# Attention scores from stacked parts, with the row's minimum as the exponential's offset

## The reference, cut to what matters

```python
s = jnp.einsum('bnqkgd,bnskd->bnkgqs', qb, kb, preferred_element_type=jnp.float32) * (HEAD_DIM ** -0.5)
s = jnp.where(mask[None, :, None, None], s + bias, NEG_INF)
sink_col = jnp.broadcast_to(sink.astype(jnp.float32).reshape(B_KV_HEADS, grp, 1, 1), s.shape[:-1] + (1,))
p = jax.nn.softmax(jnp.concatenate([s, sink_col], axis=-1), axis=-1)[..., :-1]
o = jnp.einsum('bnkgqs,bnskd->bnqkgd', p.astype(vb.dtype), vb)
```

## Time and profile before

| | |
|---|---|
| median of 3 runs | 1834.66 us (1833.57 to 1834.83) |
| the profiled execution | 1834.38 us, span 1832.6 us |
| granted TensorE clock, mean | 0.948 |
| TensorE busy with matmuls | 1627.7 us, 89% |
| DVE busy | 1338.2 us, 73% |
| ACT busy | 930.8 us, 51% |

### The profile page before, as it was taken

One profiled execution on the slowest core, in us unless ns is written; L12 is line 12 of the kernel. 1 busy time (PEld: TensorE's weight loads), 2 busy tenths in 40 slices (PEclk: granted clock), 3 DMA queues, 4 the chain that ended last, 5 costly groups with the idle time before them and its releaser, 6 DMA issues. The chain is left out here.

```text
span 1832.6 us, 28264 instructions
## 1 busy us (share of the span) xinstructions
PE 1627.7 (89%) x8048; PEld 1277.8 (70%) x8049; DVE 1338.2 (73%) x2015; ACT 930.8 (51%) x1499; POOL 307.7 (17%) x312
## 2 busy tenths in 40 slices
PE   3999888986899999991799999999999999999950
PEld 2777667874567666671678888888888888888840
DVE  5578867894578888885758977785766866656938
ACT  2312362224676666631637766573554655444728
POOL 0000100000100111113121523213122322211213
PEclk9999898997899999995899999999999999999975
DMA  7657765225733333324787989878787888776657
GB/s 303 230 195 251 254 208 192 82 81 166 307 116 116 116 115 116 105 81 174 286 332 230 393 329 364 289 281 311 237 291 251 288 296 252 265 241 197 200 152 318
DMA packets 116608, 412.84 MB, mean 225 GB/s; under 512 B 11919, under 2 KB 48015, under 8 KB 87872
## 3 DMA queue, kind: packets, MB, share of 16 engines
q1 hardware_dynamic: 95792, 342.62, 49.5%
q0 software_dynamic: 19744, 68.20, 14.6%
q10 hardware_dynamic: 1008, 1.22, 0.2%
HBM read 333.29 MB, written 80.81 MB: 226 GB/s over the span
## 5 line engine op out<-in xcount | busy, mean ns | idle before, releaser
L2025 ACT CAST gate_up_hi<-gate_up_raw 128x1024 fp32r (+1 forms) x256 | 265.7, 1053 | 91.5 <-PE psum_up L1966 65.7
L2165 DVE TENSOR_TENSOR gate_up_lo<-gate_up_raw,gate_up_hi 128x1024 fp32r<-128x1024 f32 x256 | 300.4, 1219 | 11.6 <-ACT gate_up_hi L2025 2.5
L491 PE MATMUL proj_bank<-x_hi,w_hi 128*128 128x512 f32 x448 | 182.2, 407 | 22.8 <-DVE w_lo L603 16.0
L493 PE MATMUL proj_bank<-x_hi,w_lo 128*128 128x512 f32 x448 | 177.6, 396 | 0.0
L492 PE MATMUL proj_bank<-x_lo,w_hi 128*128 128x512 f32 x448 | 177.5, 396 | 0.0
L1961 PE MATMUL psum_gate<-gate_up_hi,x_hi 128*128 128x512 f32 x392 | 158.2, 404 | 7.8 <-DVE gate_up_lo L2165 3.9
L1975 PE MATMUL psum_y<-down_hi,h_hi 128*128 128x512 f32 x392 | 158.6, 405 | 4.7 <-DVE h_lo L2165 4.7
L2165 DVE TENSOR_TENSOR down_lo<-down_raw,down_hi 128x1024 fp32r<-128x1024 f32 x128 | 150.7, 1219 | 9.0 <-ACT down_hi L2033 5.2
L669 DVE SCALAR_TENSOR_TENSOR conv<-y_win,cw,conv 128x1008 f32<-128x1008 f32 (+1 forms) x120 | 154.0, 1283 | 3.0
L1962 PE MATMUL psum_gate<-gate_up_lo,x_hi 128*128 128x512 f32 x392 | 154.1, 393 | 0.0
L1976 PE MATMUL psum_y<-down_lo,h_hi 128*128 128x512 f32 x392 | 154.0, 393 | 0.0
(11 more groups left out here) (292 smaller groups left out, 3327.8 us busy)
## 6 DMA issues: line engine op xcount, KB each, us to landing
gate_up_raw<-in_w_gate_up SPq DMA_DIRECT2D x128, 1024.0 KB, 9.4
down_raw<-in_w_down SPq DMA_DIRECT2D x64, 1024.0 KB, 6.2
x_raw<-in_ada_w SPq DMA_DIRECT2D x16, 1024.0 KB, 4.8
w_raw<-in_w_in SPq DMA_DIRECT2D x28, 512.0 KB, 5.6
x_raw<-in_xT SPq DMA_DIRECT2D x16, 512.0 KB, 9.7
q_kept<-q_stage SPq DMA_DIRECT2D x32, 256.0 KB, 2.8
q_tile<-q_kept SPq DMA_DIRECT2D x16, 512.0 KB, 4.2
wo<-w_out_kept SPq DMA_DIRECT2D x8, 1024.0 KB, 13.3
```

Source lines behind the costliest of these rows:

```text
L491: mm(bank[:, :], w_hi[side][:, k, :], x_hi[m][:, k, :], start=(k == 0), stop=False)
L493: last = mm(bank[:, :], w_lo[side][:, k, :], x_hi[m][:, k, :], start=False, stop=(k == DC - 1))
L2025: nc.scalar.copy(gu_hi[:, k, :], raw_chunk(slot, k)).then_inc(gu_high_ready, 1)
L2165: return tt(out, raw, high.bitcast(F32), ALU.subtract)
```

## The change

1. **Negated, scaled queries.** The query weights and their bias are multiplied by -1/8 where the high and low parts are made, and the table of biases by -1 instead of 8. The scores come out as minus the true ones. DVE keeps the row's minimum, started from minus the sink, and that minimum is the exponential's offset as it stands; line 1371 goes.
2. **Stacked parts.** `k_all[:, g]` now holds the high part of key head g on its own 64 partitions and its low part on the other 64. The low parts get there over a new tile `k_low` and two DMAs per key unit. The query's high part is loaded into both halves of the partitions (`q_twice`), so that one matmul with 128 contraction rows gives high·high plus high·low. Low·high stays a matmul with 64 rows.
3. **The loads of the queries** become five DMAs a tile, 768 KB instead of one of 512 KB.
4. **ACT waits** for each head's own reading of scores, not for the pair's.
5. **Memory**: `mod_rows` lies in `conv_std`, `h2T` in `x_raw`; a wait at the end of the attention stands earlier.

```diff
+QUERY_CHUNKS = slice(2 * 5, 2 * 7)
+MINUS_SCALE = -HD ** -0.5
+def load_query(sp, io, keep, t):
+    landed = keep["q_landed"][t % 2]
+    for g in range(KV_HEADS):
+        for half in range(2):
+            sp.dma_start(keep["q_twice"][HD * half:HD * half + HD, t % 2, g].rearrange("p a b -> p (a b)").bitcast(F32),
+                         io["q"][t, HD * g:HD * g + HD, 0].rearrange("p a b -> p (a b)")).then_inc(landed, 16)
+    sp.dma_start(keep["q_low"][:, t % 2].rearrange("p a b -> p (a b)").bitcast(F32),
+                 io["q"][t, :, 1].rearrange("p a b -> p (a b)")).then_inc(landed, 16)
...
+            def spread_k(n):
+                h, p, m, side = unit_of(n)
+                cols = slice(HALF * (2 * h + m), HALF * (2 * h + m + 1))
+                sp.wait_ge(dve_emptied, units_up_to(n, EMPTIED_BY_DVE))
+                for g in range(KV_HEADS):
+                    other = HD * (1 - g)
+                    sp.dma_start(k_all[other:other + HD, g, cols].bitcast(F32), k_low[HD * g:HD * g + HD, :]
+                                 ).then_inc(k_spread, 16)
...
-                low(w_lo[side][:, :, :], w_raw[side][:, :, :], w_hi[side][:, :, :].bitcast(F32)).then_inc(w_low, 1)
+                if CHUNK_KINDS[p][side] == QUERY:
+                    stt(w_lo[side][:, :, :], w_raw[side][:, :, :], MINUS_SCALE, w_hi[side][:, :, :].bitcast(F32),
+                        ALU.mult, ALU.subtract).then_inc(w_low, 1)
...
                     elif kind == KEY:
                         dve.wait_ge(kq_high, units_up_to(n, (KEY, QUERY)))
-                        stt(k_all[:, 1, cols], bank[:, :], bias, k_all[:, 0, cols].bitcast(F32), ALU.add,
-                            ALU.subtract).then_inc(dve_emptied, 1)
+                        if macro > 0:
+                            dve.wait_ge(k_spread, 32 * macro)
+                        for g in range(KV_HEADS):
+                            own = slice(HD * g, HD * g + HD)
+                            last = stt(k_low[own, :].bitcast(F32R), bank[own, :], bias[own, :],
+                                       k_all[own, g, cols].bitcast(F32), ALU.add, ALU.subtract)
+                        last.then_inc(dve_emptied, 1)
...
-                nc.scalar.copy(w_hi[side][:, :, :], w_raw[side][:, :, :]).then_inc(w_high, 1)
+                if CHUNK_KINDS[p][side] == QUERY:
+                    nc.scalar.mul(w_hi[side][:, :, :], w_raw[side][:, :, :], MINUS_SCALE).then_inc(w_high, 1)
...
-                    af(k_all[:, 0, HALF * macro:HALF * (macro + 1)], bank[:, :], ACT.Identity, bias=bias
-                       ).then_inc(kq_high, 1)
+                    for g in range(KV_HEADS):
+                        own = slice(HD * g, HD * g + HD)
+                        last = af(k_all[own, g, HALF * macro:HALF * (macro + 1)], bank[own, :], ACT.Identity,
+                                  bias=bias[own, :])
+                    last.then_inc(kq_high, 1)
...
-                for at, (ql, kl) in enumerate(((0, 0), (0, 1), (1, 0))):
-                    for g in range(KV_HEADS):
-                        rows = slice(HD * g, HD * g + HD)
-                        last = mm(S[g][:, 0:n], q[rows, t % 2, i, ql, :], k_all[rows, kl, keys],
-                                  start=(at == 0), stop=(at == 2))
-                        if at == 2:
-                            last.then_inc(scores_filled, 1)
+                for g in range(KV_HEADS):
+                    mm(S[g][:, 0:n], q_twice[:, t % 2, g, i, :], k_all[:, g, keys], start=True, stop=False)
+                for g in range(KV_HEADS):
+                    rows = slice(HD * g, HD * g + HD)
+                    mm(S[g][:, 0:n], q_low[rows, t % 2, i, :], k_all[rows, g, keys], start=False, stop=True
+                       ).then_inc(scores_filled, 1)
...
-                    ttr(probs[:, h, 0:n], S[g][:, 0:n], band_bias[:, h, band_cols(t)], 1.0, sink8[:, h:h + 1],
-                        ALU.add, ALU.max, s_max[:, h:h + 1]).then_inc(scores_read, 1)
-                dve.wait_ge(scores_read, B_HEADS * t + 2 * i + 2)
-                ts(neg_max[:, i:B_HEADS:QPAIRS], s_max[:, i:B_HEADS:QPAIRS], -HD ** -0.5, None, ALU.mult
-                   ).then_inc(neg_max_ready, 1)
+                    ttr(probs[:, h, 0:n], S[g][:, 0:n], band_bias[:, h, band_cols(t)], 1.0, minus_sink[:, h:h + 1],
+                        ALU.add, ALU.min, neg_max[:, h:h + 1]).then_inc(scores_read, 1)
...
-                act.wait_ge(neg_max_ready, QPAIRS * t + i + 1)
                 for g in range(KV_HEADS):
                     h = QPAIRS * g + i
-                    af(probs[:, h, 0:n], probs[:, h, 0:n], ACT.Exp, bias=neg_max[:, h:h + 1], scale=HD ** -0.5,
+                    act.wait_ge(scores_read, B_HEADS * t + 2 * i + g + 1)
+                    af(probs[:, h, 0:n], probs[:, h, 0:n], ACT.Exp, bias=neg_max[:, h:h + 1], scale=-1.0,
                        accum_out=p_sum[:, h:h + 1]).then_inc(exp_ready, 1)
```

54 lines of the change are left out of this document (35 added, 19 removed).

## The result

| | before | after |
|---|---|---|
| median of 6 runs each | 1834.74 us (1833.57 to 1836.87) | 1841.47 us (1839.10 to 1844.42) |
| ratio, with its 95% interval | | 1.0036 (1.0024 to 1.0048) |
| the profiled execution | 1834.38 us, span 1832.6 | 1839.10 us, span 1837.3 |

The changed kernel is slower by 6.7 us, where no change (1835.0 us) was predicted; its median lies just above the predicted range of 1828 to 1841. Its profiled execution was the fastest of the six; a second one with a trace (experiment `after_again`) took 1843.16 us.

What follows compares the result with a forecast made beforehand. TensorE bounds the full pipeline, a latency chain the attention's start, DVE the projection's stops. Terms +0.95 + 1.0 - 2.5 - 1.0 + 2.0 = +0.45 us on 1834.38 gave 1835.0 us, no change; range 1828 to 1841.

Steps and rivals of the forecast that it cites:

- The step that failed: Start of attention: five query DMAs push the output weights back by 2 us, needed only in the third tile; costed at nothing.
- The keys: Projection, DVE: low part in two instructions adds 0.66 us per key unit; three of four count, +2.0 us, bounds 0 and +3.
- The offset: ACT starts exponentials 0.65 us earlier: -2.5 us at the attention's start, -1.0 us in tiles with routing.
- The wait for the logits' copy: TensorE's 0.45 us wait for the router's logits in tiles with routing would go; 0.25 us kept for each of four.
- The inner gap: Change from stacked to half-row matmuls inside a score group idles TensorE: +1.0 us first tile, +0.95 us full pipeline.
- Six matmuls against four: Scores on TensorE: half-row matmuls already run side by side, so three streams of 384 columns before and after; saves nothing.
- The check that I had named: Sign of being right: fourth tile's first scores no more than 1 us from where they were, counted from the barrier.
- the other signs: Among them: a score group still 0.72 us to the next load, about 0.2 us idle inside, none ahead; logits' wait gone.
- the stop at `conv_mean`: Sign of being right: TensorE's stop for the convolution in the projection's second half longer by about 1.3 us.
- a third gap: Slow rival: score groups keep the entry gap and add an inner one, +11 us, 1846 us; chance 0.12.
- the other (1838.5 or more): Slow case: attention's start-up doesn't gain and keys cost 3 us; together with the three-gaps rival, chance 0.17.
- the fast rival: Half-row load hides under a stacked matmul, inner gap vanishes: -9.4 us, 1826 with DVE and ACT terms; chance 0.10.

Runs made afterwards that it cites:

- after_again: The changed kernel, unedited, run once more to get a second traced execution; median 1842.72 us, ratio 1.0037 to the kernel before.
- a_list_free: Changed kernel; GpSimd waits for the cleared expert lists to land only ahead of its first scatter, no longer ahead of the 1/std; 1836.72 us, ratio 1.0008.
- a_single_query: Changed kernel; from the third tile on, query high parts loaded into one half only, 512 KB in three transfers; 1838.95 us, ratio 1.0016.
- b_query_bytes: Kernel before plus two unused 128 KB loads a tile from the third on, `h2T` lying in `x_raw`; 1836.67 us, ratio 1.0002.
- b_stack_only: Changed kernel with parts 1 and 4 (negated, scaled queries; ACT's wait per head) undone; 1843.0 us, ratio 1.0043 to the kernel before.
- b_gate_rows: Kernel before, with GpSimd's clearing started only behind the landing of the last of the second normalisation's four rows; ratio 1.0012.
- b_offset_gate: Kernel before with parts 1 and 4, and GpSimd's clearing started behind the fourth of eight output weight pieces; 1834.58 us, ratio 0.9991.
- a_query_after_wo: Changed kernel with the third tile's query loads moved behind all pieces of the output weights; 1846.54 us, ratio 1.0054 to the kernel before.
- b_offset_only: Kernel before with only parts 1 and 4 of the change (negated, scaled queries; ACT's wait per head); 1833.69 us, ratio 0.9991.
- b_gate_later: Kernel before, with GpSimd's clearing also waiting for the second tile's input rows; ratio 0.9997.
- a_keys_one: Changed kernel with the keys' low part made by one 128-partition DVE instruction, subtracting constants; only projection read: 71.82 us from unit 36 to 48.
- a_low_first: Changed kernel with the two half-row matmuls of a group ahead of the two stacked ones; 1844.06 us, ratio 1.0043 to the kernel before.

## Why the prediction was wrong

**The step that failed** is one that I had costed at nothing: "At the start they push the output weights back by 2 us, which are needed only in the third tile." The push was there, and larger with the projection's delay: GpSimd starts 3.57 us later, of which 1.9 us counted from the first scores. But I had asked only who *multiplies* by these weights. Two more things hang on them and on their traffic: GpSimd's clearing waits for their last piece, its own 1.5 MB share the DMA engines with the larger query loads, and the 1/std stands behind it in GpSimd's queue. The row of the fourth tile's stop was in my list (1.97 us for DVE) and I had read it as DVE's queue alone; how near GpSimd's chain was to it, I did not ask. The runs that show it: without the wait, 1.0008 instead of 1.0037 (`a_list_free`); without the doubled bytes, 1.0016 (`a_single_query`, which also has fewer transfers). The bytes alone in the kernel before do not reach it (`b_query_bytes`, 1.0002); what the changed kernel adds to them (more and smaller transfers, an attention that reaches the variance sooner) was not separated. And the stack without the offset lost as much in the median while the one execution traced had no wait for the lists (`b_stack_only`), so this account covers the changed kernel and not every kernel with the stack.

**The clock.** It fell behind the stop of 2.98 us and cost 1.57 us (5.90 instead of 4.33). No term held that. Near 2 us of stop it goes either way: no fall behind 1.97 (before), 1.89 (`a_list_free`, `a_single_query`) and 2.06 (`b_gate_rows`), a fall behind 1.88 (`b_offset_gate`), 1.89 (`a_query_after_wo`), 1.98 (`b_stack_only`), 2.04 (`b_offset_only`), 2.15 (`b_gate_later`) and 2.18 us (`b_query_bytes`). The fall cost 1.5 to 1.6 us, and 2.9 and 3.0 us in `b_stack_only` and `a_query_after_wo`. Part of the spread between executions of one kernel is this.

**The keys** were right in kind and mis-sized: 0.88 us for each and not 0.66, since the two instructions take 0.75 and 0.79 us from start to start, where the one took 0.66. Predicted +2.0 us; from unit 36 to the first scores it is +1.1 to +2.3. The place was wrong. I had them last until the convolution's stop at 410.59; that stop has its old length (5.1 us), and the time is lost earlier, 1.78 us at unit 48, for the low part of the query weights. Before, that was ready at 377.16 for a use at 377.31: a margin of 0.15 us that no wait shows. In the first half the changed kernel loses too: from the start of its unit 19 to `conv_mean` it takes 46.10 and 46.99 us, before it was 44.93 (45.69 in `a_keys_one`). That does not last: unit 36, counted over both halves, starts at 304.88 and 306.83 us, before at 305.49, and it moves by as much between kernels with the old keys, so the traces give no price for it.

**The offset** was right. Predicted -2.5 us at the start, measured 28.46 to 26.53, that is -1.93 with the clock's part; predicted -1.0 in the tiles with routing, measured 252.08 to 250.92, that is -1.16 (`b_offset_only`). The wait for the logits' copy is gone as foretold.

**The inner gap** was right in kind and a little too large in size. Predicted +1.0 us in the first tile, measured +0.77 (12.91 to 13.68, `b_stack_only`) and, beside the offset, +0.58 (12.31 to 12.89); the 28.46 to 29.46 us from the first to the third tile hold the clock's return too, which came 29.0 instead of 26.6 us behind the first scores. Predicted +0.95 in the pipeline, measured 1.16 beside the offset and 0.18 without it. That a gap is hidden at a group's entry and not inside it is what `a_low_first` shows. Six matmuls against four made no difference otherwise: 252.08 us before and after. TensorEngine Tiling (Array Packing) of the Trainium skill (Key Properties) says that a switch of the tiling mode drains the array; the runs agree, with 0.17 to 0.26 us at full clock at each of two changes, wherever they are put, and at no third in the groups shown. (The row on small-K matmuls that the prediction draws on stands in the section "Why this matters for your kernels" of TensorE: Matmul & The Clock Gate of the Trainium skill.)

**The check that I had named** ("the fourth tile's first scores no more than 1 us from where they were, counted from the barrier") was too weak. Counted from the first scores they stood at 48.70 us and stand at 48.07 in one execution (right) and at 46.80 in the other (1.9 us sooner), and the loss began one pair behind it. Of the other signs, two failed: a group now takes 0.93 us to the next load and not 0.72, which the prediction's own inner gap implied, and the stop at `conv_mean` did not grow. The rivals on the slow side had the time and not the mechanism: the rows exclude a third gap (1846), and in the other (1838.5 or more) the start-up was to gain nothing, where it gained 0.6 and 1.9 us. The lower end of the range, 1828, is not halfway to the fast rival (1826) as it was said to be; that would be 1830.5.

## What to carry to other kernels

When a transfer is pushed back, list everyone who waits on its semaphore, on the idle engines too, and then what stands behind each of them in its queue: the price here was on an engine busy for 17% of the time. Ask of each stretch how full the DMA engines are before adding bytes to it (0.75 left room: bytes that raised it to 0.91 cost nothing that shows; at 0.99 the lists landed late), and judge a clearing or store by when the backlog ends, not by when it is issued. A wait for housekeeping belongs at the first use of what it guards. And compare medians before a trace of one execution: the clock alone moved single stretches by 1.3 to 3.0 us here.
